# Layer 2's attention output product as one level of Strassen, with the sums of the attended values on GpSimd

## What is computed

```python
def hybrid_layer(x, norm_g, w_in, conv_w, q_norm_g, k_norm_g, sinks,
                 w_conv_out, w_attn_out, gate_b, w_out):
    h = rms_norm(x, norm_g)
    u = jnp.einsum('bsd,dc->bsc', h, w_in)
    v_c, b_c, c_c, z_c, q, k, v, z_a, gate_logits = jnp.split(u, SPLIT_POINTS, axis=-1)
    y_c = b_c * causal_depthwise_conv(c_c * v_c, conv_w) * jax.nn.silu(z_c)
    y_a = jnp.einsum('bsc,cd->bsd', y_c, w_conv_out)
    o = sliding_window_attention(q, k, v, sinks) * jax.nn.silu(z_a)
    y_b = jnp.einsum('bsc,cd->bsd', o, w_attn_out)        # 512 x 1024 by 1024 x 1024
    gates = jax.nn.sigmoid(gate_logits + gate_b)
    g_a, g_b = jnp.split(gates, N_BRANCHES, axis=-1)
    return x + jnp.einsum('bsd,de->bse', g_a * y_a + g_b * y_b, w_out)
```

## Time and profile before

| | |
|---|---|
| median of 3 runs | 817.2 us (816.49 to 817.74) |
| the profiled execution | 816.7 us |
| its span, first to last instruction | 814.7 us |
| PE busy | 808.5 us |
| PE weight load busy | 687.1 us |
| DVE busy | 609.4 us |
| ACT busy | 321.9 us |
| POOL busy | 182.6 us |
| DMA, mean over the span | 134 GB/s |

### The profile page before, as it was taken

The page is one execution under the profiler, slowest core; times in us unless marked ns, Lnnn a source line. Parts: engine busy times, 40 slices in busy tenths (PEclk is TensorE's granted clock), DMA queues, the critical chain, the costliest instruction groups (busy, mean ns, idle before and its releaser), DMA issues.

```text
span 814.7 us, 11429 instructions
## 1 busy us (share of the span) xinstructions
PE 808.5 (99%) x4220; PEld 687.1 (84%) x4220; DVE 609.4 (75%) x1096; ACT 321.9 (40%) x701; POOL 182.6 (22%) x189
## 2 busy tenths in 40 slices
PE   9999999999999999999999999999999999999998
PEld 7778888888888888888888888888888888999986
DVE  4998778768984476885579788978952269599998
ACT  4374465632212255334445554441000122355580
POOL 2212111111111221121324445444323224000000
PEclk9999999999999999999999999999999999999999
DMA  7332214445143222653365555566876335866562
GB/s 239 87 97 77 79 52 153 158 157 179 53 155 126 82 83 77 208 175 90 91 130 130 125 119 120 128 130 155 168 165 158 104 88 145 233 182 183 182 205 78
DMA packets 129565, 108.92 MB, mean 134 GB/s; under 512 B 4525, under 2 KB 101350, under 8 KB 129510
## 3 DMA queue, kind: packets, MB, share of 16 engines
q1 hardware_dynamic: 123142, 95.60, 38.4%
q0 software_dynamic: 6336, 12.58, 9.4%
q10 hardware_dynamic: 32, 0.01, 0.0%
HBM read 106.08 MB, written 27.26 MB: 164 GB/s over the span
## 4 chain that ended last, share of the span: by engine, by line
PE 92%; DVE 5%; issue 1%; ACT 1%; DVEq 0%; ACTq 0%
PE proj L1736 24%; PE proj L1738 24%; PE proj L1737 24%; PE bank_t L1750 3%; PE bank_o L1825 2%; DVE x L1447 1%; DVE w_lo L1142 1%; PE score L1738 1%; PE score L1737 1%; PE score L1736 1%; PE score L1900 1%; PE score L1899 1%; PE score L1811 1%; PE score L1810 1%; PE bank_o L1918 1%
## 5 line engine op out<-in xcount | busy, mean ns | idle before, releaser
L723 POOL TENSOR_SCALAR w_hi<-w_raw 128x1024 fp32r<-128x1024 f32 x109 | 128.8, 1182 | 436.2 <-DMA w_raw<-in_w_in_dram 310.8
L1142 DVE TENSOR_TENSOR w_lo<-w_raw,w_hi 128x1024 fp32r<-128x1024 f32 x145 | 179.9, 1244 | 60.2 <-POOL w_hi L723 59.6
L1736 PE MATMUL proj<-xt_hi,w_hi 128*128 128x512 f32 (+1 forms) x448 | 171.1, 382 | 0.0
L1738 PE MATMUL proj<-xt_hi,w_lo 128*128 128x512 f32 (+1 forms) x448 | 168.1, 375 | 0.0
L1737 PE MATMUL proj<-xt_lo,w_hi 128*128 128x512 f32 (+1 forms) x448 | 167.8, 375 | 0.0
L1738 PEld LDWEIGHTS proj<-xt_hi,w_lo 128*128 128x128 f32 x448 | 84.4, 188 | 15.5
L1737 PEld LDWEIGHTS proj<-xt_lo,w_hi 128*128 128x128 f32 x448 | 84.5, 189 | 14.2
L1736 PEld LDWEIGHTS proj<-xt_hi,w_hi 128*128 128x128 f32 x448 | 84.5, 189 | 13.9
L1736 PE MATMUL proj<-w_hi,xt_hi 128*128 128x512 f32 x152 | 61.0, 401 | 0.2 <-ACT prob L922 0.2
L1738 PE MATMUL proj<-w_hi,xt_lo 128*128 128x512 f32 x152 | 59.5, 392 | 0.0
L1737 PE MATMUL proj<-w_lo,xt_hi 128*128 128x512 f32 x152 | 59.4, 391 | 0.0
(11 more groups left out here) (420 smaller groups left out, 1774.4 us busy)
## 6 DMA issues: line engine op xcount, KB each, us to landing
w_raw<-in_w_in_dram SPq DMA_DIRECT2D x79, 512.0 KB, 3.8
w_sums<-in_w_in_dram SPq DMA_DIRECT2D x8, 1024.0 KB, 7.5
w_raw<-w_sums SPq DMA_DIRECT2D x32, 256.0 KB, 3.3
w_raw<-in_w_out_dram SPq DMA_DIRECT2D x14, 512.0 KB, 3.3
w_raw<-in_w_in_dram SPq DMA_DIRECT2D x26, 256.0 KB, 3.6
w_sums<-w_sums POOLq DMA_DIRECT2D x6, 1024.0 KB, 9.9
w_sums<-in_w_out_dram SPq DMA_DIRECT2D x4, 1024.0 KB, 6.8
w_sums<-in_w_in_dram POOLq DMA_DIRECT2D x4, 1024.0 KB, 9.9
```

The source lines that it names most:

```text
L723: pool.tensor_scalar(hi, raw, 1.0, 1.0, ALU.mult, ALU.mult).then_inc(hi_done, 1)
L1142: dve.tensor_tensor(lo, raw, hi.bitcast(F32), ALU.subtract).then_inc(w_split, 1)
L1736: pe.matmul(out, left[0], right[0], start=first, stop=False)
L1738: return pe.matmul(out, left[1], right[0], start=False, stop=last)
```

## The change

- The product of the attended values with `w_attn_out` becomes one level of Strassen. Its 8 pieces become 14 (AOUT = 88 to COUT = 102): seven products for each of two halves of columns (`attended_product`). Each has 24 matmuls of 256 moving columns instead of 512. From COUT on all piece numbers are 6 higher.
- The results are put together by DVE (`combine_out`, 14 operations of 128x512) and ACT (`take_first_out`, 2 copies). The 8 evacuations by ACT are gone.
- The left operand needs four sums of quarters of the attended values. POOL makes them (`attended_sum`, 128x1024 each, at steps 84, 85, 85 and 86). ACT rounds three of them to `so_hi` and the fourth into a free quarter of `o2_hi`, DVE makes the low parts (`attended_low`).
- ACT makes the high part in OS in DVE's place. The quarter that no product reads is left out.
- A fourth group of weight sums, for `w_attn_out`, comes first. So 16 copies and 16 adds replace 12 and 12. The copies go after pieces 12 to 27. The adds go after pieces 53, 54, 56, 57, 59, 60, 62, 63, 65, 66, 68, 69, 71, 72, 74 and 75. Each group has a copy semaphore of its own; steps 2 and 3 wait as before.

```diff
-COPY_AT = [*range(4 * U_GA, 4 * U_O0), *range(4 * U_Z0, 4 * U_Z1)]
-SUM_AT = [4 * U_Z1 + 4 + 3 * i for i in range(4 * GROUPS)]
+COPY_AT = range(4 * U_RQK, 4 * U_O0)
+GROUP_ORDER = [ATTENDED, 0, 1, 2]
+SUM_AT = [4 * U_Z1 + 1 + 3 * i // 2 for i in range(4 * GROUPS)]
...
+SO_SUM_AT = (AOUT - 4, AOUT - 3, AOUT - 3, AOUT - 2)
+SO_HI_AT = ((AOUT - 1, 0), (AOUT - 1, 1), (AOUT, 0), (AOUT, 1))
+SO_LOW_AT = ((AOUT, 0), (AOUT, 1), (AOUT + 1, 1), (AOUT + 2, 1))
...
             def gather(i):
 
-                group, step = divmod(i, 4)
+                group, step = GROUP_ORDER[i // 4], i % 4
                 t = (0, 2, 1, 3)[step]
-                if i == 0:
-                    pool.wait_ge(w_copied, 16 * 4 * GROUPS)
+                if step == 0:
+                    pool.wait_ge(w_copied[group], 16 * 4)
                 if step >= 2:
                     pool.wait_ge(w_gathered[group], 16 * step)
...
+            def attended_sum(i):
+
+                x11, x12, x21, x22 = (quarter(gT2, row, col) for row in range(2) for col in range(2))
+                if i == 0:
+                    pool.wait_ge(o2_split, KC)
+                    pool.tensor_tensor(x22, x22, x21, ALU.subtract).then_inc(so_summed, 1)
...
+            def combine_out(x):
...
+                elif product == S1:
+                    dve.wait_ge(so_split, 4)
+                    dve.tensor_tensor(v_sum_out, w_sum, psum, ALU.add).then_inc(out_combined, 1)
...
+                elif product == S3:
+                    dve.scalar_tensor_tensor(out=out(1, 1), in0=v_sum_out, scalar=-1.0, in1=psum, op0=ALU.mult, op1=ALU.subtract).then_inc(out_combined, 1)
+                    dve.tensor_tensor(w_sum, w_sum, psum, ALU.add).then_inc(out_combined, 1)
+                    dve.wait_ge(out_combined, 7 * pair + 6)
+                    dve.tensor_tensor(out(1, 0), w_sum, kept, ALU.add).then_inc(out_combined, 1)
...
+            def attended_product(x):
...
+                left = left_of_attended(product)
+                w = [ring_parts(n, i)[0] for i in (1, 2)]
+                for j in range(2):
+                    for k in range(4):
+                        last = products(out_bank(x)[:, j, :], [t[:, k, j * P:(j + 1) * P] for t in w], [t[:, k, :] for t in left], k == 0, k == 3)
+                last.then_inc(piece_done, 1)
...
-                        if u == U_AOUT:
-                            pe.wait_ge(o2_split, KC)
                         if u == U_COUT:
                             pe.wait_ge(yc_done, KC)
+                            wait_combined_out(8 + q)
```

More of the change, by code:

```diff
@@ L446, in left_of, with sum_of_attended, left_of_attended @@
             return [t[:, chunk:chunk + 4, token:token + 256] for t in ((hi, lo), (s_hi, s_lo))[source]]
+        def sum_of_attended(product):
+            place = {S2: 0, S1: 1, S4: 2}
+            if product == S3:
+                return [quarter(t, 1, 0) for t in (o2_hi, o2_lo)]
+            return [t[:, 4 * place[product]:4 * place[product] + 4, :] for t in (so_hi, so_lo)]
+        def left_of_attended(product):
+            source, chunk, token = LEFT[product]
+            if source:
+                return sum_of_attended(product)
+            return [t[:, chunk:chunk + 4, token:token + 256] for t in (o2_hi, o2_lo)]
         def pair_of(t, c, r):
@@ L775, in _ @@
                     prepare_mask()
+                for i in range(4):
+                    if SO_SUM_AT[i] == n:
+                        attended_sum(i)
                 if n in SUM_AT:
@@ L983, in _ @@
                         gate_step(n - GATES)
-                    if half == 1 and 4 * U_COUT + 2 <= n < 4 * U_COUT + 6:
-                        q = n - 4 * U_COUT - 2
+                    if (n, half) in SO_HI_AT:
+                        product, after_sums = ((S2, 3), (S1, 1), (S4, 4), (S3, 2))[SO_HI_AT.index((n, half))]
+                        act.wait_ge(so_summed, after_sums)
+                        act.activation(sum_of_attended(product)[0], raw_sum(product), ACT.Copy).then_inc(so_hi_done, 1)
+                    if half == 1 and AOUT <= n < COUT:
+                        if (n - AOUT) % 7 == 0:
+                            take_first_out((n - AOUT) // 7)
+                    if half == 1 and COUT + 2 <= n < COUT + 6:
+                        q = n - COUT - 2
                         act.wait_ge(sx_summed, (4, 6, 8, 10)[q])
@@ L1691, in _ @@
                         left_lows(c)
[L1692 to L1695, removed]
+                    if half == 1 and AOUT <= n < COUT:
+                        combine_out(n - AOUT)
+                    if half == 1 and 0 <= n - COUT < 5:
+                        input_sums(n - COUT)
+                    if half == 1 and 0 <= n - COUT - 3 < 4:
+                        input_low(n - COUT - 3)
                     if n >= FINAL and (n - FINAL) % 2:
@@ L1717, in _ @@
                         take_tiles(n, half)
-                    if half == 1 and WIN_FIRST <= n < 4 * U_AOUT and not splits_wait(n, half):
+                    if half == 1 and WIN_FIRST <= n < AOUT and not splits_wait(n, half):
                         for m in ROUNDED_AT[n]:
                             split_piece(m)
+                    if (n, half) in SO_LOW_AT:
+                        attended_low(SO_LOW_AT.index((n, half)))
                     if (n, half) == (0, 0):
```

183 lines of the change are left out of this document (138 added, 45 removed).

## The result

The changed kernel takes 833.1 us (median; 830.92 to 837.55), the one before in the same runs 817.0 us: ratio 1.0203, 95% interval 1.0176 to 1.023. It is slower, as forecast, but by 16.1 us and not by 2. The profiled execution took 830.9 us, 829.2 of them between the first and the last instruction, 14.5 more than before.

What follows compares the result with a forecast made beforehand. PE's instruction stream was taken to bound the kernel: 816.7 - 3.5 (output product) + 0.1 (its end) + 5.2 (waits from weight sums) = 818.5, plus 0.5 to the median, 819.0 us. Range 813.8 to 825.5 us.

Steps and rivals of the forecast that it cites:

- with the row of the add that stood at the same place: Attention steps 63, 69, 75: old adds' timings priced PE's waits at AV2 at 0.6, 1.6 and 1.8 us.
- 0.4 us a group: Weight sums: allowance for adds delaying the next weight piece and for slower selects beside DVE, bringing the waits to 5.2 us.
- One block, more spare time: First group, attention step 57: one block with 1.4 us of selects meets more spare time, costing 0 to 0.5 us.
- 1.3 us of delay and 12.1 of landing: Weight sums: upper ends for the delay of step 2's issue per group and for an add's landing, in us.
- The pace: Output product: 336 matmuls at 0.119 us each, 40.0 us in all, making the stage 3.5 us shorter.
- a sign of being wrong: The prediction is wrong if AV2 starts on time (then 814 us) or if PE waits for `w_lo`.
- DVE per piece ... fit in the gaps: Output stage: DVE's split and combination take 1.9 of 2.86 us per piece; four low parts of 1.23 us fit between.
- The end of the stage: Second convolution piece waits for all of DVE's combinations: 0.1 us of loss, bounds 0 and 1.
- The sums on GpSimd: Four sums before the output product, 1.05 to 4.3 us each, cost nothing at either end.
- Weights that starve PE: Pairs of adds delay weight loads to some 16 us; PE stops 2 to 4 us more a group: 821.3 to 827, chance 0.17.
- The other rivals: Attention waits of 0 to 1.7 us (0.27) or 1.7 to 3.5 (0.12); too few output weight slots, 4 us (0.02).
- cut "to 12": Weight sums: upper bound of PE's waits, 17.5 us, reduced to 12 because a late band shifts everything behind it.

Runs made afterwards that it cites:

- the kernel before with the tight adds: Kernel before the change, its 12 adds moved to the changed kernel's first 12 places and its copies after pieces 12 to 23: 830.1 us, ratio 1.0143.
- the kernel with the late step 3: Changed kernel with four adds moved one piece later, from 57, 63, 69, 75 to 58, 64, 70, 76: 817.6 us, ratio 1.000.
- the interleaved groups: Changed kernel, same 16 add places, two groups of weight sums alternating so step 3 follows step 2 by three pieces: 821.8 us, ratio 1.0058.
- the last run: Changed kernel with each group's last add one piece later and pieces 91 to 101 rounded by ACT instead of GpSimd: 816.0 us, ratio 0.9983.
- the spread schedule: Changed kernel with the 16 adds after every third piece from 29 to 74: 837.9 us, ratio 1.0252.
- the run with the safe places: Changed kernel with adds after pieces 32, 35, 47, every third from 50 to 83, and one after the output product: 818.2 us, ratio 1.0013.

## Why the prediction was off

**The direction and the mechanism were right.** PE waits at AV2 behind POOL's band, the band starts behind an add and not behind ACT, and the places are the ones named, one group more. The same DMAs with four of them one piece later lose nothing.

**Their sizes were not.** The sum had 0 to 0.5, 0.6, 1.6 and 1.8 us for the four groups; measured were 3.53, 1.71, 2.47 and 3.63, with a fifth of 0.23. The first step that failed is "with the row of the add that stood at the same place". It took over the distance from that add's issue to AV2, and counted what could shorten it at 0.4 us a group. In the last group AV2 could have started at 559.30 - 3.63 = 555.67, 10.0 us after the issue at 545.67; before it was 545.18 - 533.95 = 11.2. That is 1.2 us. The rest is work that was a little slower: from issue to AV2 it took 13.6 us, where 13.0 was counted (the band 2.8 instead of 2.4). In the second and third groups the distance was 0.4 and 0.5 us shorter and the work 0.7 and 0.4 longer. Together the waits are 11.6 us, where the sum had 5.2.

**The first group was waved through.** "One block, more spare time" had no row behind it. The pair of adds at pieces 53 and 54 held the weight piece back, its rounding came before the band, and step 2 went out at 409.60, 10.7 us ahead of AV2's due time (423.79 - 3.53 = 420.26). It then landed after 11.6 us instead of 9.9. The forecast's own upper ends, 1.3 us of delay and 12.1 of landing, were too small for the first and nearly reached by the second, and were not applied to this group at all.

**A term was missing: the lower clock.** 3.2 us in the changed kernel. The bounds priced a wait at its length, as if it cost nothing afterwards. The Trainium skill ("TensorE: Matmul & The Clock Gate", Part 1: The HAM clock gate) says that an idle PE falls back to half of the clock; here it did so after two of five waits, and the forecast had not weighed it. The two were the longest, but in the kernel before with the tight adds it fell after waits of 1.9 to 2.6 us too.

These make the 15.85 us. A bracket counts from the end of the pipeline of the matmul before, so the starts give somewhat more than the brackets: AV2 starts 3.7, 1.9, 0.4, 2.6 and 3.8 us later after the matmul before it than in the kernel before the change, 12.4 in all. The matmuls just after a wait add about 0.1 us each time, some 0.6 in all, and the lower clock 3.2. That is 16.2 of the 16.4 us by which the stretch from the first to the last AV2 is longer. A check from the other side: the kernel with the late step 3 has a span of 816.6 and 1.5 us of such waits. 816.6 - 1.5 + 11.6 + 3.2 = 829.9, against 829.2. For the interleaved groups, 4.8 of waits and one stretch at 0.50 (562.4 to 565.5): 816.6 - 1.5 + 4.8 + 1.6 = 821.5, against 821.9.

**The product.** The pace was right (0.120 us a matmul against 0.119), and with DVE free of GpSimd the stage takes 40.3 us, where 40.0 was forecast. In the change as it was made it takes 42.1 (620.45 to 662.54, from its first matmul to the convolution product's). So it won 1.4 us instead of 3.5. PE waited for `w_lo` there, for 0.8 us, which the forecast had named as a sign of being wrong. The term that failed is "DVE per piece ... fit in the gaps": 1.9 of 2.86 us by rows in which GpSimd stood still. In the first seven pieces a split and a low part are due almost each piece, some at 2.05 us, and DVE has no gap.

**The end of the stage** was named at the right operation, at 0.1 us. It is 0.08 in the changed kernel (673.70 - 662.54 = 11.16 against 11.08), and 0.6 in the last run, where the stage runs at full pace and PE comes sooner; that is within the bounds of 0 and 1.

**The sums on GpSimd** delay nothing before the output stage and by the traces cost some tenths of a us in it, near to the forecast of nothing. Each lies between its bounds of 1.05 and 4.3 us. The estimate of 2.2 us from the Trainium skill ("GPSIMD Engine Reference", Elementwise side-by-side) was low: 2.40 to 2.83.

**The rivals.** Weights that starve PE didn't occur in the changed kernel: outside the output stage it has no wait for `w_lo`, and a load beside a pair of adds landed after 12.8 us, where this rival had some 16. Its mechanism was in the wrong place: a late piece hurts by what is queued behind its rounding and its split, on POOL in the first group, on DVE in the spread schedule. The other rivals had waits that were too short or none.

**The range** ended at 825.5 since the sum of the delays, 17.5 us, had been cut "to 12" with no row for the cut, and the clock was not in it. Uncut, it would have ended near 831, still under the median of 833.1.

## What to carry to other kernels

A wait on an in-order queue is priced by the next thing behind it that the bounding engine needs: work out its due time from the new schedule, delayed pieces included, and not from the old one's distances. Four DMA issues moved behind that one consumer were worth 15.5 us, more than four times the 3.5 us that the new product was forecast to win. In the sum of a wait of PE, a second price belongs in the upper bound, the matmuls after it at the lower clock: 1.6 us each after six of the waits of 1.9 to 3.6 us here, nothing after one of 2.47. And where two engines work side by side on SBUF, take their durations from rows in which both are busy.

## What the runs showed of the hardware

- The clock. After waits of PE of 3.53, 3.63, 2.57, 2.20, 2.15 and 1.88 us the granted clock was 0.50 for about 3.4 us each time, starting at most 1.6 us after PE had gone on; after waits of 2.47, 1.71 and 1.34 us it stayed at 1.00. In the three long waits of the spread schedule (5.8, 4.4 and 4.7 us) it fell while PE still stood, at 249.9, 311.3 and 359.1, and came back at 256.7, 318.2 and 366.0, after some 6.9 us each time. So the length of the wait alone doesn't say it, and what else does stays open.
- DVE's two-input operations of 128x1024 take 1.22 us alone, 2.05 beside a rounding on GpSimd and 3.30 beside one of its sums (616.52), and POOL's rounding 1.05 alone and up to 1.9 in the same stretch. With the rounding on ACT both splits and low parts in the output stage are at 1.22. That it is GpSimd beside it and not the load of the stage follows from this pair of runs; the path by which they hinder each other was not tried. The Trainium skill ("GPSIMD Engine Reference", 1. Specifications) names contention of the two engines for SBUF where DVE reads two SBUF inputs, and the splits and low parts are such operations; these rows agree.
- A sum of two 128x1024 float32 operands takes GpSimd 2.40 to 3.35 us (3.35 in the run with the safe places), and the same four sums take DVE 1.21 to 2.07.
- In the changed kernel an add of 1 MB took 8.2 to 11.6 us to land, and 13.1 to 14.2 as the second of a pair; a weight load issued beside a pair took 12.8.
